# The second attention of a two-block kernel: scores two pairs ahead in an idle accumulator, probabilities normed before their transposes, whole units of projection between pairs

## The chip, the cores and the metric

One core of one Trainium2 chip. The metric is the device time of one execution in microseconds (us), lower is better. Three executions of the kernel before took 921.38, 922.76 and 923.89 us, median 922.76.

## The reference, cut to what matters

Two transformer blocks in float32 run one after the other on 256 tokens of 1024 features. The second one begins with a projection `proj = h @ w_in + b_in` (3584 columns), and has two attentions over it, with 8 query heads and 2 key heads of 64 features each. Both see 256 own tokens and 256 context tokens, so 512 keys.

```python
s = einsum(q, k) * 64 ** -0.5                # 128 queries x 512 keys for each head
# A: windowed, with a sink            B: global
m = max(max(s), sink)                 # p = softmax(s)
e = exp(s - m)
p = e / (sum(e) + exp(sink - m))
o = einsum(p, v)
out = (sigmoid(g_a) * (o_a @ w_branch_a) + sigmoid(g_b) * (o_b @ w_branch_b)) @ w_out
```

The gate logits g_a and g_b are the last 2048 columns of the projection. They are not needed by the attention, so their part of the projection can be computed beside it.

## The kernel before, in words

**Weights and units.** Every weight matrix is walked in panels of 512 columns (`panels`, L84), and a panel in units of 256 rows. For each unit SyncE loads `raw` (a ring of 4), ScalarE rounds it to `whi` (L1411), VectorE subtracts to get `wlo` (L1952), and TensorE multiplies with the two as `unit` (L760) says: 12 matmuls of 128x512 for 256 tokens, high times high, high times low, low times high. ScalarE and VectorE each write their splits into their own instruction order with `ahead(pos)` (L1415, L1957): all splits up to unit pos + 3 that are not yet issued come at this place of the program. Panels alternate between the two accumulators `acc[0]` and `acc[1]` (two PSUM banks each; `Plan.bank`, L119). The first unit of a panel waits until the panel before it in the same accumulator is evacuated (`panel_out`). For the panels IN3 to IN6 (gate logits) VectorE does that in `biased` (L1979), which first calls `ahead` for the panel's last unit.

**The attention stage.** 16 pairs: branch A has pairs 0 to 7, branch B pairs 8 to 15; a pair is two heads times 128 queries. For each pair TensorE makes scores (L1258) into `scores0` and `scores1`, VectorE masks (A alone), takes the maximum and scales it (L2647, L2648, L2651 or L2312), ScalarE takes the exponentials with their sum (L1802 for the sink in A, L1804), TensorE transposes the probabilities (L875), ScalarE copies the transposes out (`t_out`, L1468), and TensorE multiplies them with the values (L1269). Transposes and values use two PSUM banks `turned0` and `turned1` in strict turn: the list `t_names` (L168) gives each use its bank, and a use waits until the one two places before it is copied out (`t_begin`, L805). Before the change the order in that list is, for pair p: PT(2p), PT(2p+1), O(p). Four small matmuls (L1273) broadcast the inverse sums of the pair into the bank of O(p); VectorE copies them out (L2663) and multiplies them into the values (L2664, into `oabT`). After four pairs `oabT` is split into high (ScalarE, L1831) and low (VectorE, L2668) for the panels BA0 to BB1.

**Order of the work.** Each engine's program is written by hand, and each runs in its order. The three functions called `attend_pairs` (L858 TensorE, L1492 ScalarE, L2136 VectorE) hold the loops. Between the pairs TensorE runs one unit per pair of the panels IN3 to IN6, BA0, BA1 (`AB_FILL`), in two halves of 128 tokens (`ab_fill`): one ahead of values(p), one behind. `ab_units(j)` = min(18, j + 2) says how many units are done at pair j; units 18 and 19 come after the loop. `AB_TURNS` names further transposes between pairs: the keys and queries of branch B (kB.0, kB.1, qB.0, qB.1 at pairs 4, 5, 6) and rows of gate1 (pairs 9, 10). GpSimd squares, norms and turns B's queries and keys meanwhile.

Of the kernel before, what the change touches and what calls it, by code (L numbers as in the profile page):

```python
# [100 lines left out]

NARROW = dict(MK0=H_MEM * DQ_MEM, AQ=GATE_RANK + H_MEM * DQ_MEM, CK=KV_RANK + ROPE)


class Plan:


    def __init__(self):
        self.no, self.unit, self.landed, self.cols = {}, {}, [], []
        loads = [0] * RING  # L110
        for i, (name, kts, per_unit) in enumerate(panels()):
            self.no[name], self.unit[name] = i, len(self.landed)
            for u in range(len(self.landed), len(self.landed) + kts // UNIT):
                loads[u % RING] += 16 * per_unit
                self.landed.append(loads[u % RING])
                self.cols.append(NARROW.get(name, COLS))
        self.units = len(self.landed)

    def bank(self, name):  # L119

        return self.no[name] % 2, self.no[name] // 2
# [13 lines left out]
AB_TURNS = {4: ("kB.0",), 5: ("kB.1",), 6: ("qB.0", "qB.1"), 9: ("gate1.0",), 10: ("gate1.1",)}  # L135
MOD_CTX = 4
# [10 lines left out]
AB_LAST = 2  # L147
# [7 lines left out]
def ab_units(j):  # L155

    return min((4 * KT + 2 * KT // 2) // UNIT - AB_LAST, j + 2)

# [9 lines left out]
def t_names():  # L168
# [11 lines left out]
    out += pairs_t("AB", AB_PAIRS, {p: list(v) for p, v in AB_TURNS.items()})  # L180
# [17 lines left out]
def pairs_t(name, n, extra={}, ahead={}):  # L198

    out = []  # L200
    for p in range(n):
        out += [f"{name}.PT{2 * p}", f"{name}.PT{2 * p + 1}"] + ahead.get(p, []) + [f"{name}.O{p}"] + extra.get(p, [])
    return out
# [5 lines left out]
             + [f"MLA.{i}" for i in range(H_MLA)] + [f"AB.{i}" for i in range(2 * HEADS * T)])  # L209
# [30 lines left out]
def hybrid_kernel(nc, a, out):  # L240

    ctx = ExitStack()
    with ctx:
# [15 lines left out]
        sc = [ctx.enter_context(nc.psum_tensor(f"scores{i}", [P, COLS], F32)) for i in range(2)]  # L259

# [120 lines left out]
        oabT = sb("oabT", [P, KT, SEQ], F32, three)  # L381
        inverse_row = sb("inverse_row", [P, P], F32, three)
# [16 lines left out]
        s_full = [sem(f"scores_full{i}") for i in range(2)]  # L399
        s_free = [sem(f"scores_free{i}") for i in range(2)]  # L400
# [56 lines left out]
        def normed(t):  # L457

            room = oabT[:, 4 * t + 2:4 * t + 4, :].rearrange("p a b -> p (a b)")
# [282 lines left out]
        def _(pe):  # L742
# [115 lines left out]
            def attend_pairs(name, n, scores, blocks, values, fill_units, after=None, fill_rest=None):  # L858
# [8 lines left out]
                if fill_rest:  # L867
                    fill_rest(0)
# [9 lines left out]
                for p in range(n):  # L878
                    turned_out(p, 0)
                    if fill_rest:  # L880
                        turned_out(p, 1)
                    if p + 1 < n:
                        score(p + 1)
                    if not fill_rest:
                        turned_out(p, 1)
# [6 lines left out]
                    if fill_rest:  # L892
                        fill_rest(p + 1)
                    if after:
                        after(p)
# [358 lines left out]
            def ab_scores(p, banks):  # L1254
# [3 lines left out]
                return [pe.matmul(banks[e][:, :], qT[br][64 * e:64 * e + 64, hp, P * t:P * t + P],  # L1258
                                  kT[br][64 * e:64 * e + 64, 2 * hp // GROUP, :], start=True, stop=True)
                        for e in range(2)]  # L1260

            def ab_values(p, bank):
                br, hp, t = ab_pair(p)
                group = HD * (2 * hp // GROUP)
                for kt in range(4):
                    v = qkv[:, kt, 768 * br + 640:768 * br + 768] if kt < 2 else \
                        kvx[:, kt - 2, 256 * br + 128:256 * br + 256]
                    for e in range(2):
                        pe.matmul(bank[HD * e:HD * e + HD, 0:P], v[:, group:group + HD],  # L1269
                                  probT[:, e, P * kt:P * kt + P], start=(kt == 0), stop=(kt == 3))  # L1270
                pe.wait_ge(ev("ab_sums"), p + 1)
                for e in range(2):
                    ins = pe.matmul(bank[HD * e:HD * e + HD, P:2 * P],  # L1273
                                       soft[:, (2 * p + e) % 4, 8:9].broadcast_to([P, HD]), ident[:],
                                    start=True, stop=True)
                return ins

            def ab_unit(j, tokens=range(T)):

                if j < 16:  # L1280
                    unit(AB_FILL[j // 4], j % 4, lta, tokens=tokens)
                    return
                if j == 16 and 0 in tokens:
                    lt_wait("oab", 1)
                unit(AB_FILL[4 + (j - 16) // 2], j % 2, ltb, first_kt=2 * (j % 2), tokens=tokens,
                     low=("oab", 1) if j == 16 and 0 in tokens else None)

            def ab_fill(p, tokens):
                for j in range(ab_units(p - 1) if p else 0, ab_units(p)):
                    ab_unit(j, tokens)  # L1290
# [12 lines left out]
            def ab_turn(i, j):  # L1303
                for name in AB_TURNS.get(i, ())[j:j + 1]:
# [8 lines left out]
            def ab_rest(p):  # L1313
                if p > 0:
                    ab_turn(p - 1, 0)
                ab_fill(p, (1,))

            attend_pairs("AB", AB_PAIRS, ab_scores, 4, ab_values, lambda p: ab_fill(p, (0,)), after=lambda p: ab_turn(p, 1),
                         fill_rest=ab_rest)


            ab_unit(18)
# [72 lines left out]
        def _(act):  # L1395
# [96 lines left out]
            def attend_pairs(name, n, exps, first, units, blocks, between=None, after=None):  # L1492
# [11 lines left out]
                for p in range(n):  # L1504
# [6 lines left out]
                    if between:  # L1511
                        between(p)
# [4 lines left out]
                    if after:  # L1517
                        after(p)
# [280 lines left out]
            def ab_exps(i, slot, row, bank):  # L1799
                br, h = i // (HEADS * T), 2 * (i % (HEADS * T) // (2 * T)) + i % 2  # L1800
                if br == 0:
                    act.activation(soft[:, row, 6:7], GAIN["attn_sink_2"][:, h:h + 1], ACT.Exp,  # L1802
                                   bias=soft[:, row, 2:3], scale=-1.0)
                return act.activation(prob[:, slot, :], bank[:], ACT.Exp, bias=soft[:, row, 2:3],  # L1804
                                      scale=HD ** -0.5, accum_out=soft[:, row, 4:5])

            def ab_out(i, j):
                for name in AB_TURNS.get(i, ())[j:j + 1]:
# [8 lines left out]
            def ab_between(i):  # L1817
                if i == 1:
                    sqrt("ab", stat[:, 2:4, :])
                ab_out(i, 0)  # L1820

            def ab_after(i):
                ab_out(i, 1)
                if i % AB_SPAN == 0 and i > 0:
                    oab_hi(i // AB_SPAN - 1)

            def oab_hi(g):

                b, k = T_USE[f"AB.O{AB_SPAN * (g + 1) - 1}"]
                act.wait_ge(t_free[b], k + 2)  # L1830
                act.copy(ltb[0][:, 2 * g:2 * g + 2, :], oabT[:, 2 * g:2 * g + 2, :]).then_inc(lt_hi, 1)  # L1831

            attend_pairs("AB", AB_PAIRS, ab_exps, PLAN.unit["IN3"], ab_units, 4, ab_between, ab_after)
            gate2_sigmoid(0)
            oab_hi(3)
# [94 lines left out]
        def _(dve):  # L1930
# [205 lines left out]
            def attend_pairs(name, n, maxima, sums, weigh, first, units, after=None, early_sums=False,  # L2136
                             before_maxima=None, before_weighing=None):
# [10 lines left out]
                def inverses(p):  # L2148
# [5 lines left out]

                ahead(first)
                softmax(0)
                for p in range(n):
                    if early_sums:
                        inverses(p)
                    ahead(first + units(p))  # L2160
                    if before_maxima:
                        before_maxima(p)
                    if p + 1 < n:
                        softmax(p + 1)
                    if not early_sums:
                        inverses(p)
                    if before_weighing:
                        before_weighing(p)
# [3 lines left out]
                    if after:  # L2172
                        after(p)
# [458 lines left out]
            def norm_sums(t):  # L2632
                for v, s, _, square in normed(t):
# [6 lines left out]
            def ab_step(i):  # L2640
                return i // (HEADS * T), 2 * (i % (HEADS * T) // (2 * T)) + i % 2, i // 2 % T

            def ab_maxima(i, s, bank):
                br, h, t = ab_step(i)
                if br == 0:
                    far = bank[:, P * (1 - t):P * (1 - t) + P]
                    done(dve.tensor_tensor(far, far, (keep_past if t == 0 else keep_next)[:], ALU.add))  # L2647
                done(dve.tensor_reduce(s[:, 0:1], bank[:], AX.X, ALU.max))  # L2648
# [281 lines left out]
```

## Time and profile before

| | |
|---|---|
| median of 3 executions | 922.76 us |
| the profiled execution, its own time | 922.41 us |
| its span in the trace | 920.8 us |
| TensorE (PE) matmul busy | 899.3 us, 98% |
| VectorE (DVE), ScalarE (ACT), GpSimd (POOL) busy | 720.8, 551.3, 162.2 us |
| mean granted TensorE clock | 0.998 |
| attention stage, first scores to the end of unit 19 | 563.80 to 682.95 us |

The span is the time between the first and the last instruction that the profiler recorded; 1.6 us of the execution lie around it. A duration of a matmul contains its way through the array, so matmuls that follow one another overlap in the table: what a group costs is the distance between the start of its first and the start of the next group.

### The profile page before, as it was taken

Reading aid. Unit: us, or ns where it says so; the run is one execution under the profiler, and the core shown is the slowest. Engines: PE = TensorE matmul, PEld = TensorE weight load, DVE = VectorE, ACT = ScalarE, POOL = GpSimd, SP = SyncE. Lnnn points to the kernel's source line nnn. Section 1 sums busy time; section 2 is a strip of 40 time slices with the busy share of each in tenths; the row PEclk is TensorE's granted clock in tenths of the full one; section 3 lists DMA queues with packets and bytes.
Section 4 is the critical chain, followed back from the end, with each engine's and each line's share of the span. In section 5 each row is a group of like instructions: output and inputs, shape, how many; then the busy total and the mean of one; then the engine's idle time right before and its main releaser. Section 6 shows DMA issues by size and latency. Waiting matters only on the chain.

```text
span 920.8 us, 13753 instructions
## 1 busy us (share of the span) xinstructions
PE 899.3 (98%) x4732; PEld 729.8 (79%) x4732; DVE 720.8 (78%) x1046; ACT 551.3 (60%) x863; POOL 162.2 (18%) x247
## 2 busy tenths in 40 slices
PE   8999999999999999999999999999999999999996
PEld 6888888777878778888888887666678688888885
DVE  4779476878878778887779798865668889999976
ACT  6775755476776576777333445755664766666633
POOL 8000000215600000110112001640000023344400
PEclk9999999999999999999999999999999999999999
DMA  9756844876653447887699655322246456555572
GB/s 322 203 151 202 278 138 120 284 275 202 175 177 112 128 143 255 269 287 259 211 330 334 211 177 196 98 80 82 80 148 191 146 179 182 178 171 179 173 245 82
DMA packets 100538, 176.20 MB, mean 191 GB/s; under 512 B 8561, under 2 KB 36593, under 8 KB 100353
## 3 DMA queue, kind: packets, MB, share of 16 engines
q1 hardware_dynamic: 93120, 149.87, 50.7%
q0 software_dynamic: 7184, 25.50, 8.3%
q8 instruction: 34, 0.56, 0.2%
q14 instruction: 24, 0.19, 0.1%
q10 hardware_dynamic: 176, 0.08, 0.0%
HBM read 174.38 MB, written 1.05 MB: 191 GB/s over the span
## 4 chain that ended last, share of the span: by engine, by line
PE 57%; DVE 5%; ACT 2%; issue 1%; DMA 1%; DVEq 0%
PE acc L783 39%; PE acc L1160 3%; PE acc L1165 2%; PE scores L1160 2%; PE turned L1160 2%; PE turned L1269 2%; PE scores L1258 1%; PE turned L875 1%; DVE wlo L1952 1%; PE turned L1371 1%; PE turned L1165 1%; PE scores L1165 1%; PE turned L1185 1%; PE turned L819 1%; DMA raw<-in_w_out 1%
## 5 line engine op out<-in xcount | busy, mean ns | idle before, releaser
L1952 DVE TENSOR_TENSOR wlo<-raw,whi 128x1024 fp32r<-128x1024 f32 (+3 forms) x269 | 346.0, 1306 | 91.0 <-ACT whi L1411 80.7
L1411 ACT CAST whi<-raw 128x1024 fp32r<-128x1024 f32 (+3 forms) x269 | 273.3, 1032 | 150.8 <-PE acc L783 99.6
L783 PE MATMUL acc<-whi,lta 128*128 128x512 f32 (+2 forms) x896 | 227.9, 392 | 0.2 <-DVEq L2529 0.2
L783 PEld LDWEIGHTS acc<-whi,lta 128*128 128x128 f32 x896 | 160.2, 188 | 43.4 <-issue 10.4
L783 PE MATMUL acc<-wlo,lta 128*128 128x512 f32 (+2 forms) x448 | 121.2, 383 | 0.0
L665 POOL DMA_DIRECT2D wm<-in_w_mod x48 | 34.4, 719 | 422.6 <-DVEq L2083 239.7
L783 PEld LDWEIGHTS acc<-wlo,lta 128*128 128x128 f32 x448 | 82.9, 188 | 16.9
L783 PE MATMUL acc<-whi,ltb_hi 128*128 128x512 f32 (+1 forms) x268 | 73.3, 392 | 1.7 <-ACT whi L1411 0.8
L783 PE MATMUL acc<-wlo,ltb_hi 128*128 128x512 f32 (+1 forms) x268 | 71.1, 384 | 1.6 <-DVE wlo L1952 1.6
L783 PE MATMUL acc<-whi,ltb_lo 128*128 128x512 f32 (+1 forms) x268 | 71.5, 385 | 0.1
L783 PEld LDWEIGHTS acc<-wlo,ltb_hi 128*128 128x128 f32 x268 | 49.4, 188 | 12.0 <-DVE wlo L1952 2.0
L783 PEld LDWEIGHTS acc<-whi,ltb_lo 128*128 128x128 f32 x268 | 49.3, 188 | 11.4 <-DVE ltb_lo L2783 1.4
L783 PEld LDWEIGHTS acc<-whi,ltb_hi 128*128 128x128 f32 x268 | 47.8, 188 | 13.2 <-issue 2.7
L724 POOL TENSOR_TENSOR conv<-conv 128x512 f32<-128x512 f32 x6 | 7.8, 1294 | 166.3 <-DVEq L2832 166.3
L1160 PE MATMUL acc<-lta,whi 128*128 128x512 f32 x128 | 35.0, 395 | 0.0
L783 PE MATMUL acc<-whi,ff_hi 128*128 128x512 f32 x128 | 35.0, 395 | 0.0
L783 PE MATMUL acc<-whi,ff_lo 128*128 128x512 f32 x128 | 34.2, 389 | 0.0
L783 PE MATMUL acc<-wlo,ff_hi 128*128 128x512 f32 x128 | 34.2, 389 | 0.0
L1468 ACT ACTIVATE probT<-turned 128x512 f32<-128x512 f32 (+1 forms) x44 | 23.7, 581 | 17.6 <-PE turned L875 11.2
L783 PEld LDWEIGHTS acc<-whi,ff_lo 128*128 128x128 f32 x128 | 24.0, 188 | 5.0
L783 PEld LDWEIGHTS acc<-wlo,ff_hi 128*128 128x128 f32 x128 | 24.0, 188 | 5.0
L2081 DVE SCALAR_TENSOR_TENSOR turn<-wm,sic,turn 128x512 f32<-128x512 f32 x35 | 26.2, 749 | 1.1
(387 smaller groups left out, 1437.0 us busy)
## 6 DMA issues: line engine op xcount, KB each, us to landing
raw<-in_w_in SPq DMA_DIRECT2D x88, 512.0 KB, 4.2
wm<-in_w_mod POOLq DMA_DIRECT2D x48, 512.0 KB, 6.5
raw<-in_w_up SPq DMA_DIRECT2D x88, 256.0 KB, 3.0
raw<-in_w_up SPq DMA_DIRECT2D x32, 512.0 KB, 4.7
raw<-in_w_down SPq DMA_DIRECT2D x32, 512.0 KB, 5.2
raw<-in_w_down SPq DMA_DIRECT2D x44, 256.0 KB, 3.1
raw<-in_w_o SPq DMA_DIRECT2D x8, 512.0 KB, 4.5
raw<-in_w_out SPq DMA_DIRECT2D x8, 512.0 KB, 4.3
```

The lines of the kernel that those rows point to most:

```text
L665: pool.dma_start(wm[:, k], rows(a["w_mod_2"], k)[:, :, bass.ds(COLS * c, COLS)])\
L783: ins = pe.matmul(acc[s][:, t, 0:n], lhs[part][:, kt0 + kk, tok], w[:, u % RING, kk, 0:n], start=(opens and k == 0 and kk == 0 and j == 0) ...
L819: ins = pe.transpose(bank[:, 256 * kk + P * t:256 * kk + P * t + P], src[:, t, c:c + P], ident[:])
L875: ins = pe.transpose(bank[:, P * j:P * j + P], prob[:, e, P * j:P * j + P], ident[:])
L1160: pe.matmul(up_bank(c, f), whi[:, u % RING, kk, P * f:P * f + P], lta_parts[:, :, UNIT * k + kk], start=(k == 0 and kk == 0), stop=False)
L1165: ins = pe.matmul(up_bank(c, f)[:, 0:SEQ], wlo[:, u % RING, kk, P * f:P * f + P], lta_parts[:, 0, UNIT * k + kk], start=False, stop=(k == ...
L1185: ins = pe.matmul(bank[:, 2 * j:2 * j + 1], src[:, P * j:P * j + P], one_col[:], start=True, stop=True)
L1269: pe.matmul(bank[HD * e:HD * e + HD, 0:P], v[:, group:group + HD], probT[:, e, P * kt:P * kt + P], start=(kt == 0), stop=(kt == 3))
L1411: act.copy(whi[:, s, :, 0:n], raw[:, s, :, 0:n]).then_inc(hi_ready, 1)
L1468: act.activation(dst, tb[b][0:(parts or P), 0:n], ACT.Copy, scale=scale).then_inc(t_free[b], 1)
L1952: dve.tensor_tensor(wlo[:, s, :, 0:n], raw[:, s, :, 0:n], whi[:, s, :, 0:n].bitcast(F32), ALU.subtract)\
L2081: done(dve.scalar_tensor_tensor(total, w, factor, total, ALU.mult, ALU.add))
```

## The change

It concerns the attention stage alone.

- Panels IN3 to IN6 and BA0 all go into `acc[0]`. The two banks of `acc[1]` become `scores2` and `scores3`. Scores of pair p use banks 0, 1 or 2, 3 in turn, and are made at pair p - 2; those of pair 1 wait for the evacuation of IN2 from `acc[1]`.
- VectorE multiplies each row of probabilities by its inverse sum in place (`ab_norm`, two `tensor_scalar` of 128x512 for each pair) before TensorE transposes them. The matmuls of L1273, the copy L2663 and the product L2664 go, and so does `oabT`.
- ScalarE rounds O(p) from PSUM to `ltb[0]` (`ab_hi`) and VectorE subtracts to `ltb[1]` (`ab_low`), 128x128 for each pair, in place of four times 128x512.
- values(p-1) comes after the transposes of pair p and the scores of pair p + 2. The order of the `turned` banks becomes PT(2p), PT(2p+1), O(p-1), then extra transposes.
- TensorE runs whole units: `ab_units(j)` = min(19, j + 3).
- `prob` and `probT` get a second copy each.
- The norm sums of B's keys and queries move ahead of the loop, and sqrt("ab") ahead of the copies of pair 0.

```diff
+BESIDE_SCORES = ("IN3", "IN4", "IN5", "IN6", "BA0")
...
+            s = 0 if name in BESIDE_SCORES else i % 2
+            self.banks[name] = s, filled[s]
...
+AB_LATE = 6
-AB_LAST = 2
+AB_LAST = 1
...
-    return min((4 * KT + 2 * KT // 2) // UNIT - AB_LAST, j + 2)
+    return min((4 * KT + 2 * KT // 2) // UNIT - AB_LAST, j + 3)
...
+    for p in range(AB_PAIRS):
+        out += [f"AB.PT{2 * p}", f"AB.PT{2 * p + 1}"] + ([f"AB.O{p - 1}"] if p else []) + list(AB_TURNS.get(p, ()))
...
+        sc += [acc[1][:, t] for t in range(T)]
```

TensorE:

```diff
+            ab_scores(0)
+            s, k = PLAN.bank("IN2")
+            pe.wait_ge(panel_out[s], k + 2)
+            ab_scores(1)
+            ab_fill(0)
+            for p in range(AB_PAIRS):
+                ab_turned(p)
+                if p + 2 < AB_PAIRS and p != AB_LATE:
+                    ab_scores(p + 2)
                 if p > 0:
+                    ab_values(p - 1)
+                ab_turn(p)
+                ab_fill(p + 1)
+                if p == AB_LATE:
+                    ab_scores(p + 2)
+            ab_values(AB_PAIRS - 1)
             ab_unit(19)
```

`ab_turned` waits for `ab_normed` of each head; `ab_values` waits for the copies of its own pair and, in `t_begin`, for its bank.

ScalarE:

```diff
+            ahead(PLAN.unit["IN3"])
+            ab_exp(0)
+            ab_exp(1)
+            sqrt("ab", stat[:, 2:4, :])
+            for p in range(AB_PAIRS):
+                for e in range(2):
+                    t_out(f"AB.PT{2 * p + e}", ab_probT[p % 2][:, e, :])
+                if p > 0:
+                    ab_hi(p - 1)
+                ahead(PLAN.unit["IN3"] + ab_units(p))
+                ab_out(p)
+                if p + 2 < AB_PAIRS:
+                    ab_exp(p + 2)
+            ahead(PLAN.unit["IN3"] + ab_units(AB_PAIRS))
+            ab_hi(AB_PAIRS - 1)
             gate2_sigmoid(0)
```

VectorE (`IN_DONE` is 1, 5, 9, 13 after the change):

```diff
+            def ab_norm(p):
+                for e in range(2):
+                    b, k = S_USE[f"AB.{2 * p + e}"]
+                    dve.wait_ge(s_free[b], k + 2)
+                s = ab_rows(p)
+                if p < AB_PAIRS // 2:
                     done(dve.tensor_tensor(s[:, :, 4:5], s[:, :, 4:5], s[:, :, 6:7], ALU.add))
                 done(dve.reciprocal(s[:, :, 8:9], s[:, :, 4:5]))
+                for e in range(2):
+                    row = ab_prob[p % 2][:, e, :]
+                    dve.tensor_scalar(row, row, s[:, e, 8:9], None, ALU.mult).then_inc(ev("ab_normed"), 1)
...
+            ahead(PLAN.unit["IN3"])
+            ab_maxima(0)
+            norm_sums(0)
+            ab_norm(0)
+            norm_sums(1)
+            var(stat[:, 2:4, :], HD).then_inc(ev("ab_var"), 1)
+            ab_maxima(1)
+            for p in range(AB_PAIRS):
+                if p in IN_DONE:
+                    c = IN_DONE.index(p)
+                    biased(f"IN{3 + c}", gate2[:, :, COLS * c:COLS * c + COLS])
+                if p + 1 < AB_PAIRS:
+                    ab_norm(p + 1)
+                if p == 0:
+                    inverse("ab", stat[:, 2:4, :])
+                    dve.sem_inc(ev("ab_inverse"), 1)
+                ahead(PLAN.unit["IN3"] + ab_units(p))
+                if p == AB_LATE:
+                    ab_low(p - 1)
+                if p + 2 < AB_PAIRS:
+                    ab_maxima(p + 2)
+                if p > 0 and p != AB_LATE:
+                    ab_low(p - 1)
```

## Rows read from the trace of the kernel before

**Rows 1.** The page, parts 1 and 2: busy engines, granted clock in 40 slices.

```profile
PE 899.3 (98%) x4732; PEld 729.8 (79%) x4732; DVE 720.8 (78%) x1046; ACT 551.3 (60%) x863; POOL 162.2 (18%) x247
...
PEclk9999999999999999999999999999999999999999
```

**Rows 2.** The timeline of PE, one pair: start us, us, engine line op, names, shape, count.

```profile
571.42 1.13 PE L1258 MATMUL scores<-kT_a,qT_a 64*128 64x512 f32 x4
572.48 1.20 PE L783 MATMUL acc<-whi,lta 128*128 128x512 f32 x4
...
574.07 0.66 PE L1269 MATMUL turned<-probT,qkv 128*64 128x128 f32 x8
574.56 0.61 PE L1269 MATMUL turned<-probT,kvx 128*64 128x128 f32 x8
574.99 0.39 PE L1273 MATMUL turned<-ident,soft 128*64 128x128 f32 x4
575.31 1.21 PE L783 MATMUL acc<-whi,lta 128*128 128x512 f32 x4
...
576.83 1.03 PE L875 MATMUL turned<-ident,prob 128*128 128x128 f32 x8
577.79 1.13 PE L1258 MATMUL scores<-kT_a,qT_a 64*128 64x512 f32 x4
```

**Rows 3.** The timeline of PE at the stage's two ends (unit 19 begins at 680.23).

```profile
563.80 1.13 PE L1258 MATMUL scores<-kT_a,qT_a 64*128 64x512 f32 x4
...
680.23 1.07 PE L783 MATMUL acc<-whi,ltb_hi 128*128 128x512 f32 x4
...
682.95 1.07 PE L783 MATMUL acc<-whi,ltb_hi 128*128 128x512 f32 x4
```

**Rows 4.** The timeline of DVE, parts of pairs 3 and 9.

```profile
590.39 1.22 DVE L1984 TENSOR_TENSOR gate<-acc,bias 128x1024 f32<-128x1024 f32 x1
591.84 0.25 DVE L2657 TENSOR_TENSOR soft<-soft 128x2 f32<-128x2 f32 x1 [0.22 <-DVE gate L1984]
...
592.44 1.23 DVE L1952 TENSOR_TENSOR wlo<-raw,whi 128x1024 fp32r<-128x1024 f32 x1
593.58 0.29 DVE L2647 TENSOR_TENSOR scores<-scores,keep_past 128x128 f32<-128x128 f32 x1
...
595.95 0.28 DVE L2663 COPY inverse_row<-turned 128x128 f32<-128x128 f32 x1
...
622.29 0.68 DVE L2648 TENSOR_REDUCE soft<-scores 128x1 f32<-128x512 f32 x1
...
623.79 0.15 DVE L2312 TENSOR_SCALAR soft<-soft 128x1 f32<-128x1 f32 x1
```

**Rows 5.** The timeline of ACT.

```profile
578.62 1.28 ACT L1462 ACT_TABLE_LOAD   x1
...
588.96 0.29 ACT L1802 ACTIVATE soft<-gains,soft 128x1 f32<-128x1 f32 x1 [0.22 <-DVE soft L2651]
...
589.73 0.19 ACT L1804 ACTIVATION_READ_ACCUMULATOR prob<-scores,soft 128x1 f32 x1
589.82 1.03 ACT L1411 CAST whi<-raw 128x1024 fp32r<-128x1024 f32 x1
591.11 1.08 ACT L1468 ACTIVATE probT<-turned 128x512 f32<-128x512 f32 x2 [0.26 <-PE turned L875]
```

**Rows 6.** Groups by line and shape: count | busy us, mean ns | idle before.

```profile
L1744 ACT COPY probT<-turned 128x256 f32<-128x256 f32 x8 | 2.7, 398 | 0.0
...
L2079 DVE TENSOR_SCALAR turn<-wm,sic 128x512 f32<-128x512 f32 x5 | 2.4, 481 | 0.0
```

**Rows 7.** The timeline of DVE at the stage's start: first maxima, first norm sum, their variance.

```profile
566.39 0.30 DVE L2647 TENSOR_TENSOR scores<-scores,keep_past 128x128 f32<-128x128 f32 x1
...
575.97 0.67 DVE L2634 TENSOR_REDUCE stat<-oabT 128x8 f32<-128x512 f32 x1
...
578.68 0.18 DVE L2060 TENSOR_SCALAR stat<-stat 128x32 f32<-128x32 f32 x1
```

More of the change, by code:

```diff
@@ L119, in bank @@
     def bank(self, name):
[L121 removed]
+        return self.banks[name]
 PLAN = Plan()
@@ L208 @@
              + [f"gla.{s}.{t}" for s in range(1, 8) for t in range(T)]
-             + [f"MLA.{i}" for i in range(H_MLA)] + [f"AB.{i}" for i in range(2 * HEADS * T)])
+             + [f"MLA.{i}" for i in range(H_MLA)])
+MLA_SCORES = {b: 1 + max(k for c, k in S_USE.values() if c == b) for b in range(2)}
+for i in range(2 * HEADS * T):
+    b = i % 4
+    S_USE[f"AB.{i}"] = b, i // 4 + MLA_SCORES.get(b, 0)
 COLUMNS = (("g_mem", 8), ("g_mix", 8), ("g_ffn", 8), ("g_ckv", 2), ("c_2", 8), ("c_ctx_2", 8),
@@ L1489, in attend, with attend_pairs @@
                         after(i)
-            def attend_pairs(name, n, exps, first, units, blocks, between=None, after=None):
+            def attend_pairs(name, n, exps, first, units, blocks, after):
                 def exp(p):
@@ L1797, in _, with ab_exp, ab_out @@
             keys_out(0)
[L1799 to L1808, printed above, removed]
+            def ab_exp(p):
+                br, hp, _ = p // (HEADS // 2 * T), p % (HEADS // 2 * T) // T, p % T
+                for e in range(2):
+                    g = STEPS["AB"][0] + 2 * p + e
+                    b, _ = S_USE[f"AB.{2 * p + e}"]
+                    row = soft[:, g % 4]
+                    act.wait_ge(soft_ready, g + 1)
+                    if br == 0:
+                        act.activation(row[:, 6:7], GAIN["attn_sink_2"][:, 2 * hp + e:2 * hp + e + 1], ACT.Exp,
+                                       bias=row[:, 2:3], scale=-1.0)
+                    act.activation(ab_prob[p % 2][:, e, :], sc[b][:], ACT.Exp, bias=row[:, 2:3],
+                                   scale=HD ** -0.5, accum_out=row[:, 4:5]).then_inc(s_free[b], 1)
+            def ab_out(p):
+                for name in AB_TURNS.get(p, ()):
                     g = int(name[-1])
@@ L1815, in ab_out, with ab_hi @@
                         queries_out(1, (g,))
[L1817 to L1833, printed above, removed]
+            def ab_hi(p):
+                br, hp, t = p // (HEADS // 2 * T), p % (HEADS // 2 * T) // T, p % T
+                b, k = T_USE[f"AB.O{p}"]
+                act.wait_ge(t_full[b], k + 1)
+                act.copy(ltb[0][:, 4 * br + hp, P * t:P * t + P], tb[b][:, 0:P])\
+                   .then_inc(lt_hi if p % AB_SPAN == AB_SPAN - 1 else ev("oab_hi"), 1)
+            ahead(PLAN.unit["IN3"])
[3 more added lines that the diff above has]
+            for p in range(AB_PAIRS):
+                for e in range(2):
+                    t_out(f"AB.PT{2 * p + e}", ab_probT[p % 2][:, e, :])
[7 more added lines that the diff above has]
+            ab_hi(AB_PAIRS - 1)
             gate2_sigmoid(0)
-            oab_hi(3)
             for n in (1, 2, 3):
@@ L2134, in attend, with attend_pairs @@
                         after(i)
-            def attend_pairs(name, n, maxima, sums, weigh, first, units, after=None, early_sums=False,
-                             before_maxima=None, before_weighing=None):
+            def attend_pairs(name, n, maxima, sums, weigh, first, units, after, before_weighing):
                 def rows_of(p):
@@ L2146, in softmax @@
                         maxima(2 * p + e, rows_of(p)[e], sc[b]).then_inc(soft_ready, 1)
-                def inverses(p):
+                ahead(first)
+                softmax(0)
+                for p in range(n):
+                    ahead(first + units(p))
+                    if p + 1 < n:
+                        softmax(p + 1)
                     for e in range(2):
@@ L2153, in inverses @@
                     sums(p, soft[:, r:r + 2])
[L2155 to L2168, printed above, removed]
+                    before_weighing(p)
                     b, k = T_USE[f"{name}.O{p}"]
@@ L2637, in _ @@
             done(dve.tensor_scalar(GAIN["attn_sink_2"], GAIN["attn_sink_2"], -1.0, None, ALU.mult))
[L2640 to L2648, printed above, removed]
-                if br == 0:
-                    return dve.tensor_scalar(s[:, 2:3], s[:, 0:1], -HD ** -0.5, GAIN["attn_sink_2"][:, h:h + 1],
-                                             ALU.mult, ALU.min)
-                return neg(s, 1, HD ** -0.5)
```

173 lines of the change are left out of this document (83 added, 90 removed).

## The prediction, made before the changed kernel was run

> **What bounds the kernel now.** I read the busy shares first: TensorE's matmuls fill 98% of the span, with the granted clock at its upper level, 2.4 GHz, in all 40 slices [rows 1]. So time is won only where TensorE has less to do or waits less, and each new wait of TensorE goes straight into the time. The timeline of PE then shows what one pair costs: transposes 0.96 us (576.83 to 577.79), scores 1.06, half a unit 1.59, values 0.92, the broadcast of inverse sums 0.32, the other half 1.52; together 6.37 [rows 2]. The groups follow one another without a gap, so the stage, 563.80 to the end of unit 19 at 682.95, is 119.15 us of nearly pure TensorE work [rows 3]. Last I read the timelines of DVE and ACT for the price of their steps [rows 4 to 7]. Neither sets the pace now: VectorE is busy 78% and ScalarE 60% of the span [rows 1].
>
> **What goes.** The broadcast: 16 x 0.32 = 5.1 us of TensorE. Two half units cost 3.11, a whole one 2.72 where units follow one another (680.23 to 682.95) [rows 2, 3]; between other work I give it 2.8, so 16 x 0.3 = 4.8. If TensorE still sets the pace, that is 9.9 us won.
>
> **What comes, and what each step costs.** Scores, maxima, exponentials and transposes keep their counts. New on VectorE for each pair: two scalings of 128x512, 0.48 each in the same form, 0.8 for both as neighbours overlap [rows 6], and the low part of 128x128, priced as the copy of that shape that goes, 0.28 [rows 4]. New on ScalarE: the high part, 128x128 out of PSUM, which no row has. It lies between 0.19, a reading of one column [rows 5], and 0.40, a copy of twice the size [rows 6]; I take 0.27. A handover between engines I take as 0.05, an estimate; the longest in the rows is 0.23 (591.61 to 591.84) [rows 4]. Loads: no DMA is added, moved past another or removed; a load waits for the low split of its slot, four units ahead of its own use, and that stays.
>
> What decides is order. I followed the three programs for one step p, counting what each instruction stands behind:
>
> - ScalarE: copies of PT(2p), PT(2p+1); high(p-1); high split of unit p+5; exponentials p+2.
> - VectorE: norm(p+1); low split of unit p+5; maxima p+2; low(p-1).
> - TensorE: transposes p; scores p+2; values p-1; unit p+3.
>
> Two things follow. High(p-1) waits for values(p-1), and the split queued behind it on ScalarE needs nothing of it but comes later by it; VectorE's low split waits for that one, and the maxima are queued behind the low split. And the bank of O(p-1), freed by low(p-1) behind the maxima, is the one that the second transposes of pair p+1 write. That closes a ring with one turn for each pair: second transposes 0.48, scores 1.06, values 1.10 until their last result (574.07 to 575.17) [rows 2], handover 0.05, high part 0.27, high split 1.03 [rows 5], handover 0.05, low split 1.14, maxima of branch A 2.37 (593.58 to 595.95), low part 0.28 and 0.1 to free the bank [rows 4]: **7.9 us for each pair, where it takes 6.37 now**. In branch B the maxima need no mask and no sink: 1.6 (622.29 to the end of the second scaling) [rows 4], so 7.2. Making scores two pairs ahead doesn't open the ring, since the transposes two places further need a bank of this one.
>
> **The evacuations.** With all gate panels in one accumulator, units 4, 8, 12 and 16 wait for the evacuation of the panel that ended just before. `biased` stands in steps 1, 5, 9, 13, and its own `ahead` puts the low split of unit p+5 ahead of it. So from the start of values: 1.10, high part, high split, low split, 1.22 of evacuation [rows 2, 4, 5] are 4.9, against 0.92 of values that TensorE has to do: a wait of 4.0 at each. Then norm(p+1), which else hides in the wait for ScalarE, comes behind it: 1.45 to the next instruction [rows 4] and 1.2 (B: 1.0) for the norm make these steps 10.6 and 9.6.
>
> **The start.** VectorE: first maxima from 566.39 [rows 7] to 568.8; three norm sums, half of 575.97 to 578.68 [rows 7], 570.1; norm of pair 0, 571.3; the other sums, 572.8; maxima of pair 1, 575.2. ScalarE: the exponentials, 0.95 for the second head (588.96 to 589.92), 576.2; table load 1.28 and root 0.2, 577.7; two copies 1.1, 578.8; high split of unit 3, 579.8 [rows 5]. Low split, 581.0. TensorE has done two scores, three units, the transposes of pair 0 and scores 2 by 576.7 and waits 4.3 for unit 3. Splits 3 to 5, maxima, exponentials and the copy that frees the bank of values(0) end at 587.4, and there values(0) begin.
>
> **The sum.** Values to values: step 1 10.6; 7.9; 7.9; 8.4 with a key copy of 0.5 on ScalarE; step 5 10.6; then the late scores, where queries turned wait for low(5) (4.1 behind values), a unit, scores 8, their maxima, exponentials and a copy follow one another, 11.8: 57.2. Branch B: 7.2, 7.2, 10.1 (step 9, with a gate copy), 7.7, 7.2, 7.2, 9.6, and two steps without maxima, 5.3 and 3.9: 65.4. So values(15) begin at 587.4 + 57.2 + 65.4 = 710.0, and unit 19 ends 3.6 later, 713.6 in place of 682.95: +30.7. Behind it, the merge of BA0 now frees the accumulator of BB0 and waits for the first gate sigmoid, queued behind high(15): from 711.4, table load 1.28, sigmoid 1.06 (as a 128x1024 split), merge 1.22, 715.0: +1.3. Sum: **+32 us**. The profiled execution took 922.4, its span 920.8 and 1.6 around it, and stands 0.3 below the median: 922.4 + 32 = 954.
>
> GpSimd's squares and norms start no later than now, since the root comes earlier, and end before the keys are wanted; if they were late, pair 4 would wait instead of running in the ring.
>
> **Rivals.** *The ring doesn't bind and TensorE sets the pace: faster.* It decides if splits run ahead of the values they are queued behind, for example if the cursor of `ahead` stands one unit further than I count. For it: TensorE's own work falls to about 5.8 for a pair, under all that VectorE has (maxima 2.37, split 1.14, norm 1.2, low 0.3: 5.0). Against it: the order is in the program. 922.4 - 9.9 + 0.5 (scores 1 wait for IN2) = 913.
>
> *Only the start, the four evacuations and the late scores wait, ordinary steps don't:* 4.3 + 4 x 4.0 + 4 - 9.9 = +14, so 937. The same cursor, wrong in one place only.
>
> *The ring, and the clock on top.* Here TensorE would stand still about 4 us five times. The page's clock line shows no slice below the upper level, and no row has a standstill of that length, so no row prices it. If it fell to 1.2 GHz at all five and each took one unit of 2.72 [rows 3] at half speed, that adds 13.6: 968. The Trainium skill (TensorE: Matmul & The Clock Gate, "HAM oscillation — how this bites in real kernels") warns that gaps in which TensorE idles bring its clock down. By that rule the time would be 968; no run shown here can bear it out.
>
> *No change within 0.3%* (about what a measurement of this kernel can tell): the gain of 9.9 would have to meet losses of the same size; no mechanism of mine gives that.
>
> **How the numbers follow.** Ring with evacuations, 0.73, 954, own range 948 to 961: the high part between its bounds moves 14 steps by -1.1 to +1.8, handovers of 0.1 add 4, overlaps I missed take 5. Clock on top 0.10; only the single waits 0.06; faster 0.09; same 0.02. The range 944 to 968 takes in the first two, with some room below for waits that are partly hidden, and leaves out the other three, 0.17. Faster 0.09, same 0.02, slower 0.89.
>
> **What would show it.** In the trace of the changed kernel: scores of neighbouring pairs 7.9 apart in A and 7.2 in B; PE idle before the second transposes (2.0 in A, 1.3 in B, ended by VectorE's low part); before unit 3 (by a split) and before units 4, 8, 12, 16 (by the evacuation), about 4 each; in all some 40 us of PE idle in the stage, and VectorE waiting for `whi`, ScalarE for O(p-1). Pairs 5.8 apart without idle time would prove the ring wrong; long matmuls behind the 4 us waits would be the clock.

## The result, and the profile after

The changed kernel takes 965.14 us (median of 4 executions, 962.28 to 967.48), the kernel before on the same chip 922.75 (4 executions, 921.38 to 923.89): **slower by 4.6%**, ratio 1.0456, 95% interval 1.0439 to 1.0473. The forecast was 954, its range 944 to 968. So the sign and the range held, and the size is nearer to the rival with the clock on top (968) than to the likeliest case. That case, the ring without the clock, had a range of its own, 948 to 961, and the run lies outside it; the wider range held because it took in the rival.

The page of the changed kernel, its span and its parts 1 and 2, against [rows 1]:

```profile
span 964.5 us, 13613 instructions
...
PE 910.3 (94%) x4668; PEld 740.3 (77%) x4668; DVE 729.1 (76%) x1058; ACT 553.5 (57%) x875; POOL 162.6 (17%) x247
...
PE   8999999999999999999999997777889999999996
...
PEclk9999999999999999999999997888989999999998
```

TensorE has 64 matmuls fewer and yet 11 us more busy time, and its share falls from 98% to 94%. Of the six slices in a row in which it is busy 7 or 8 tenths, five show the granted clock below the upper level; before, no slice did [rows 1]. Two losses lie in the same stretch: TensorE waits, and it is slow behind the waits.

The waits of PE in the stage (what waited, for whom: us in total, times, longest):

```profile
PE turned L1273 <- DVE ltb_lo L2701: 10.4, 8, 1.9
PE acc L796 <- DVE gate L2010: 9.9, 3, 3.7
PE acc L796 <- issue: 3.8, 1, 3.8
PE turned L1287 <- ACT probT_odd L1486: 3.7, 3, 2.3
PE acc L796 <- ACT whi L1429: 3.0, 1, 3.0
PE turned L1238 <- DVE ltb_lo L2701: 2.3, 1, 2.3
```

The first row is the ring of the prediction: second transposes behind the low part. The next two are the four evacuations (the fourth, before unit 16, has no releaser in the records, but VectorE's evacuation of IN6 ended just before it, at 704.4), the fourth row is values behind their copies (2.26 of it before values(0)), the fifth the start, the last the late scores. They sum to 33 us, where the prediction had 40.

The timeline of PE of one turn of the ring in branch B, against [rows 2]:

```profile
656.48 0.63 PE L1273 MATMUL turned<-ident,prob 128*128 128x128 f32 x4 [1.03 <-DVE ltb_lo L2701]
657.04 1.13 PE L1264 MATMUL scores<-kT_b,qT_b 64*128 64x512 f32 x4
658.10 0.66 PE L1287 MATMUL turned<-probT_odd,qkv 128*64 128x128 f32 x8
...
663.63 0.63 PE L1273 MATMUL turned<-ident,prob_odd 128*128 128x128 f32 x4 [1.01 <-DVE ltb_lo L2701]
664.19 1.13 PE L1264 MATMUL acc<-kT_b,qT_b 64*128 64x512 f32 x4
```

Scores follow scores after 7.15 us (657.04 to 664.19), where the prediction had 7.2 and the kernel before 6.37. In branch A the turn from 599.30 to 607.24 took 7.94 with the clock up (7.9 said); the two after it took 9.11 and 8.38, with slow matmuls in them. The other engines in the same turn, ACT and then DVE, against [rows 5] and [rows 4]:

```profile
659.24 0.27 ACT L1843 CAST ltb_hi<-turned 128x128 fp32r<-128x128 f32 x1 [1.32 <-PE turned L1287]
659.40 1.05 ACT L1429 CAST whi<-raw 128x1024 fp32r<-128x1024 f32 x1
```

```profile
660.48 1.23 DVE L1978 TENSOR_TENSOR wlo<-raw,whi 128x1024 fp32r<-128x1024 f32 x1 [2.32 <-ACT whi L1429]
661.62 0.68 DVE L2670 TENSOR_REDUCE soft<-scores 128x1 f32<-128x512 f32 x1
...
663.13 0.15 DVE L2327 TENSOR_SCALAR soft<-soft 128x1 f32<-128x1 f32 x1
663.20 0.28 DVE L2701 TENSOR_TENSOR ltb_lo<-turned,ltb_hi 128x128 fp32r<-128x128 f32 x1
```

Read in order of time the ring closes: values from 658.10, high part at 659.24, high split, low split at 660.48, maxima, low part at 663.20, transposes at 663.63. ScalarE stood idle 1.32 us and VectorE 2.32 in it: no engine is full, all three take turns.

Then two of the four evacuations, the timeline of PE before units 8 and 12, and unit 16 behind the fourth:

```profile
632.17 3.52 PE L796 MATMUL acc<-whi,lta 128*128 128x512 f32 x8 [3.12 <-DVE gate L2010]
...
636.46 1.03 PE L1273 MATMUL turned<-ident,prob 128*128 128x128 f32 x8
...
670.04 3.78 PE L796 MATMUL acc<-whi,lta 128*128 128x512 f32 x8 [3.12 <-DVE gate L2010]
...
675.33 1.47 PE L1273 MATMUL turned<-ident,prob 128*128 128x128 f32 x8
...
704.52 2.04 PE L796 MATMUL acc<-whi,ltb_hi 128*128 128x512 f32 x4 [3.75 <-issue]
...
709.78 1.32 PE L1273 MATMUL turned<-ident,prob 128*128 128x128 f32 x8
```

A unit took 4.3 us (632.17 to 636.46) and twice 5.3, where one at full speed takes 2.72 [rows 3]. The same in stretches (us; busy time of each engine with its instructions; then the granted clock):

```profile
577.00:584.00 7.00, 4.03 (x11) 3.17 (x12) 5.26 (x6) 6.08 (x8) 5.15 (x5) 0.76 0.11 18
...
650.00:660.00 10.00, 8.01 (x60) 5.86 (x61) 5.04 (x12) 5.80 (x14) 0.00 (x0) 1.00 0.16 53
670.00:680.00 10.00, 9.96 (x47) 7.47 (x48) 3.81 (x11) 3.71 (x8) 0.00 (x0) 0.69 0.15 51
680.00:700.00 20.00, 16.81 (x108) 11.47 (x108) 10.89 (x24) 10.78 (x24) 0.00 (x0) 1.00 0.23 79
```

In 670 to 680 TensorE is busy all the time and gets 47 matmuls done at 0.69; in 650 to 660 it is busy 8 of 10 us and does 60 at 1.00.

The stage's end, the timeline of PE, against [rows 3]:

```profile
721.72 1.20 PE L796 MATMUL acc<-whi,ltb_hi 128*128 128x512 f32 x4
...
725.90 1.16 PE L796 MATMUL acc<-whi,ltb_hi 128*128 128x512 f32 x4 [1.17 <-issue]
```

Unit 19 begins at 721.72, and with its 2.72 ends at 724.4, 41.5 us later than the 682.95 of before; the wait for the accumulator of BB0 behind it is 1.17 (1.3 said). Together 42.7, which is the whole difference of the medians, 42.4.

### The profile page after: what moved, and what is told of

It reads as the page before. It is cut to its first block, busy times and chain, and to the rows that moved or that the text cites. A ratio compares the mean times of both kernels' runs of the same rounds, so it can differ in the third digit from the quotient of the medians.

```text
span 964.5 us, 13613 instructions
## 1 busy us (share of the span) xinstructions
PE 910.3 (94%) x4668; PEld 740.3 (77%) x4668; DVE 729.1 (76%) x1058; ACT 553.5 (57%) x875; POOL 162.6 (17%) x247
## 4 chain that ended last, share of the span: by engine, by line
PE 53%; DVE 8%; ACT 4%; issue 2%; DMA 1%; DVEq 0%; ACTq 0%
PE acc L796 37%; PE acc L1164 3%; DVE wlo L1978 3%; PE turned L1287 2%; ACT whi L1429 2%; DVE soft L2670 2%; PE acc L1169 2%; PE scores L1164 2%; PE turned L1164 2%; PE turned L1273 1%; PE turned L1389 1%; PE turned L1169 1%; PE scores L1169 1%; PE scores L1264 1%; PE acc L1264 1%
## 5 line engine op out<-in xcount | busy, mean ns | idle before, releaser
L796 PE MATMUL acc<-whi,lta 128*128 128x512 f32 (+2 forms) x896 | 231.3, 400 | 13.2 <-DVE gate L2010 9.9
L796 PEld LDWEIGHTS acc<-whi,lta 128*128 128x128 f32 x896 | 166.6, 194 | 49.7 <-DVE gate L2010 10.7
L796 PEld LDWEIGHTS acc<-whi,ff_hi 128*128 128x128 f32 x128 | 23.4, 188 | 4.4
```

What stands on the lines that cost most here:

```text
L796: ins = pe.matmul(acc[s][:, t, 0:n], lhs[part][:, kt0 + kk, tok], w[:, u % RING, kk, 0:n], start=(opens and k == 0 and kk == 0 and j == 0) ...
```

## The experiments

All are edits of the changed kernel. The first four ran beside 7 executions of the kernel before (median 922.87), the other four beside 9 (923.58).

**The high split ahead of the high part.** The ring says that the split on ScalarE comes late only because it stands behind a wait for values(p-1). Here it is moved ahead of that wait, still behind the copies.

```diff
                     t_out(f"AB.PT{2 * p + e}", ab_probT[p % 2][:, e, :])
+                ahead(PLAN.unit["IN3"] + ab_units(p))
                 if p > 0:
                     ab_hi(p - 1)
-                ahead(PLAN.unit["IN3"] + ab_units(p))
```

> Edit: ScalarE's high split of the next unit stands ahead of high(p-1) in each step; nothing else. Ring theory: the high split no longer waits for values(p-1), so about 1.3 us drop out of the ring (values to the high part, 1.10 + 0.05 + 0.27, are then beside the split). Ordinary pairs 6.7 apart in branch A and 5.9 in B (7.9 and 7.2 in the changed kernel), waits before units 4, 8, 12, 16 of 2 to 3 us in place of 3.1 to 3.7. The stage ends 17.5 us earlier, and with shorter waits some of the clock's share of about 10 us comes back: 939 to 948 in all. Rival (the added work on VectorE, the two scalings of each pair, sets the pace): VectorE's program is untouched, so no change, 965. Rival (only the five single waits cost): ordinary pairs keep their distance, at most 4 us come back.

Measured: 940.84 (940.11 to 941.30), 1.0196 of before, interval 1.0179 to 1.0213. One line moved takes back 24 us. Waits of PE in the stage:

```profile
PE turned L1287 <- ACT probT_odd L1486: 4.9, 3, 3.5
PE acc L796 <- DVE gate L2010: 4.5, 3, 1.7
PE turned L1273 <- DVE ltb_lo L2701: 3.4, 4, 1.4
```

The low part's 10.4 fell to 3.4 and the evacuations' 9.9 to 4.5. One place in a queue fed both. The 24 us are the ring and the clock together: the same 4668 matmuls kept TensorE busy for 897.5 us here and for 910.3 in the changed kernel.

**The high split first in the step**, ahead of the copies too.

```diff
             for p in range(AB_PAIRS):
+                ahead(PLAN.unit["IN3"] + ab_units(p))
                 for e in range(2):
                     t_out(f"AB.PT{2 * p + e}", ab_probT[p % 2][:, e, :])
                 if p > 0:
                     ab_hi(p - 1)
-                ahead(PLAN.unit["IN3"] + ab_units(p))
```

> Edit: ScalarE's high split of the next unit stands first in each step, ahead of the copies of the transposes, as in the kernel before. Ring theory: the split waits for nothing of this step. Pairs 5.9 apart in both branches (TensorE's own work), waits before units 4, 8, 12, 16 under 1 us, what is left are the start (3 to 5 us) and the late scores (10.6 for that pair). The stage ends 26 us earlier, the clock stays up nearly everywhere: 926 to 934. Rival (VectorE's added work sets the pace): no change, 965. Rival (one accumulator for all gate panels is what costs): the waits before units 4, 8, 12, 16 stay over 3 us and the gain stays under 15.

Measured: 933.98 (933.37 to 934.48), 1.0121, interval 1.0104 to 1.0138. The timeline of PE, scores of three neighbouring pairs:

```profile
661.20 1.13 PE L1264 MATMUL acc<-kT_b,qT_b 64*128 64x512 f32 x4
...
667.13 1.13 PE L1264 MATMUL scores<-kT_b,qT_b 64*128 64x512 f32 x4
...
673.06 1.13 PE L1264 MATMUL acc<-kT_b,qT_b 64*128 64x512 f32 x4
```

These pairs of branch B are 5.93 apart, with no idle time: less than the 6.37 of before. This is the gain that the prediction gave the change if TensorE set the pace (5.8). In B it exists; the order of ScalarE's program hid it. In A the ordinary pairs are 6.5 to 7.3 apart, where 5.9 was expected in both branches.

**The evacuation first.** `biased` of IN3 to IN6 without the split of its own `ahead`; ScalarE as in the changed kernel.

```diff
 # in biased(): the wait for the panel's last unit, without ahead()
+                if name in BESIDE_SCORES:
+                    dve.wait_ge(unit_used, RING + last_unit(name) + 1)
+                    p, n = acc[PLAN.bank(name)[0]], n_gate[name]
+                else:
+                    p, n = panel_wait(name), n_gate[name]
-                p, n = panel_wait(name), n_gate[name]
```

> Edit: the evacuation of IN3 to IN6 no longer puts VectorE's low split of the next unit ahead of itself. Ring theory: the evacuations run in the time in which VectorE waits for ScalarE's split, the waits before units 4, 8, 12, 16 go, and the ordinary pairs stay 7.9 and 7.2 apart. Stage 10 us shorter by the waits; the clock, which fell after these waits, stays up, another 5 to 9: 945 to 951. Rival (one accumulator is the cost whatever the order, since the evacuation takes 1.2 us between two units): waits over 1 us stay, gain under 5.

Measured: 950.93 (949.53 to 951.82), 1.0303, interval 1.0283 to 1.0322. Waits of PE in the stage:

```profile
PE turned L1273 <- DVE ltb_lo L2705: 17.1, 12, 2.2
```

No unit waits for `gate` any more, but 12 transposes now wait for the low part where 8 did, 6.7 us more in all. The steps with an evacuation have become ordinary turns of the ring. 14 us come back.

**TensorE kept busy in the long waits.** The scores of pair p + 2 are made four times in steps 0, 1, 5, 9 and 13, the same numbers written each time, so 60 more matmuls stand where TensorE would idle. (`ab_scores` gets two switches for it, `first` and `last`: whether it waits for its banks and whether it announces the scores.) If time is lost to the wait alone, this costs or changes nothing; if the clock behind it costs, it comes back.

```diff
+                again = p in (0, 1, 5, 9, 13)
                 if p + 2 < AB_PAIRS and p != AB_LATE:
-                    ab_scores(p + 2)
+                    ab_scores(p + 2, last=not again)
                 if p > 0:
                     ab_values(p - 1)
                 ab_turn(p)
+                for n in range(3 if again else 0):
+                    ab_scores(p + 2, first=False, last=n == 2)
```

> Edit: in steps 0, 1, 5, 9, 13 the scores of pair p + 2 are made four times over, three of them in the wait of about 4 us that follows, and announced after the last; results the same. TensorE has 15 more pairs of score matmuls, 16 us of work, all inside the five long waits. Clock theory: the clock stays at the upper level, units behind the waits take 2.8 us and not 4 to 5, and the time falls to about 955 (the 954 of the sum without the clock). Rival (the long matmuls behind the waits are no clock but late operands or an artefact): no gain, 965 or more. If announcing the scores later is on the path, up to 2 us of the gain are lost.

Measured: 958.82 (956.52 to 962.03), 1.0383, interval 1.0359 to 1.0407: 6.3 us less than the changed kernel, by doing more. The timeline of PE at the first two long waits, and at the one before unit 12:

```profile
580.06 2.11 PE L796 MATMUL acc<-whi,lta 128*128 128x512 f32 x8 [0.47 <-ACT whi L1436]
...
588.85 0.66 PE L1291 MATMUL turned<-probT,qkv 128*64 128x128 f32 x8 [3.54 <-ACT probT_odd L1493]
...
590.15 4.22 PE L1266 MATMUL acc<-kT_a,qT_a 64*128 64x512 f32 x12
594.29 2.11 PE L796 MATMUL acc<-whi,lta 128*128 128x512 f32 x8
...
671.91 2.11 PE L796 MATMUL acc<-whi,lta 128*128 128x512 f32 x8 [0.35 <-DVE gate L2017]
```

The first two units are at full speed, the eight high matmuls in 2.11 where the changed kernel needed 3.23 and 3.78. Where TensorE still stood, 3.54 before values(0), it was slow behind it: twelve scores took 4.22, against 1.06 for four at full speed [rows 2]. In branch B, where the repeated scores filled the two long waits, values 8 to 9 took 10.0 us and values 12 to 13 took 9.1; the changed kernel took 12.5 and 11.8, and the sum of the prediction, which has no clock in it, says 10.1 and 9.6. That 6.3 us came back and not the 10 that were expected has its place in branch A: there the clock fell in three ordinary turns, behind waits of 2.37, 1.83 and 1.90, and values 1 to 4 took 28.6 us where the changed kernel took 26.1.

**Both orders**, the second and the third edit together.

> Edit: the two orders of before together: ScalarE's high split first in each step, and the evacuation without the low split ahead of it. Ring theory: stage 3 us shorter than with the first alone (933.98), since the waits of 1 us before units 4 and 16 and their followers go; 928 to 932, and still above the kernel before, because the start (about 5 us) and the late scores (about 4) are paid whatever the order, which eats the 10 us that TensorE's lighter pairs give. Rival (the lighter pairs win once nothing waits): under 920.

Measured: 931.55 (930.77 to 933.48), 1.0084, interval 1.0071 to 1.0098. Of the third edit's 14 us only 2.4 are left once the split is early (3.4 by the ratios, since the two runs stood beside other executions of the kernel before): the two edits take away the same lateness.

**Both orders, and the start mended.** What is left stands at the start and at the late scores: values(0) waited 5.2 us in the run above. Here the exponentials of pairs 2 and 8 go behind the copies of the next step, the root to step 1 with its inverse, and the gate sigmoid of BA0 one step earlier.

```diff
-            sqrt("ab", stat[:, 2:4, :])
+            late = (0, AB_LATE)
...
                     t_out(f"AB.PT{2 * p + e}", ab_probT[p % 2][:, e, :])
+                if p - 1 in late:
+                    ab_exp(p + 1)
...
+                if p == 1:
+                    sqrt("ab", stat[:, 2:4, :])
-                if p + 2 < AB_PAIRS:
+                if p + 2 < AB_PAIRS and p not in late:
                     ab_exp(p + 2)
+                if p == AB_PAIRS - 2:
+                    gate2_sigmoid(0)
...
-            gate2_sigmoid(0)
```

> Edit: as both orders together, and besides: in steps 0 and 6 ScalarE's exponentials of pair p + 2 move behind the copies of step p + 1; the root for B's norms moves to step 1; the first gate sigmoid moves ahead of the last pair's copies. Ring theory: the first values begin 5 us earlier, values 6 some 2 us, and the wait of 1.2 us before BB0 goes. By the same adding of steps the stage ends within 1 us of the kernel before: 921 to 926, verdict same. Rival (something of the change costs that is no order, e.g. contention on PSUM or SBUF): 928 or more, with matmuls or copies longer than in the kernel before.

Measured: 928.36 (927.65 to 929.98), 1.0055, interval 1.0042 to 1.0069. Better by 3.2, and 2 above what was expected. The timeline of PE shows where, and the stretches beside it how the clock went:

```profile
592.19 1.09 PE L1273 MATMUL turned<-ident,prob 128*128 128x128 f32 x4 [3.39 <-DVE ltb_lo L2710]
593.21 2.08 PE L1264 MATMUL scores<-kT_a,qT_a 64*128 64x512 f32 x4
```

```profile
589.00:592.00 3.00, 0.00 (x0) 0.00 (x0) 2.86 (x8) 1.08 (x4) 2.77 (x4) 1.00 0.39 106
592.00:596.00 4.00, 3.81 (x20) 2.00 (x22) 3.03 (x6) 2.76 (x6) 3.61 (x6) 0.57 0.30 117
```

The wait has moved from values(0) to the second transposes of pair 2, behind the low part of pair 0: VectorE is busy 2.86 of the 3.00 us, so here it does set the pace. The kernel is still slower than before by 0.55%.

The rival of this run, a cost that is no order, had 928 or more, and its time came. Its sign, longer matmuls or copies, came in part. The copies of the transposes last 0.60 us as in the kernel before, but VectorE's instructions are longer where GpSimd works beside them, on the norms of B's keys and queries. The timeline of DVE in this run:

```profile
578.29 3.49 DVE L1983 TENSOR_TENSOR wlo<-raw,whi 128x1024 fp32r<-128x1024 f32 x3
...
587.37 2.12 DVE L1983 TENSOR_TENSOR wlo<-raw,whi 128x1024 fp32r<-128x1024 f32 x1
```

The three low splits took 3.49 us with GpSimd idle from 577 to 584; the single one took 2.12, where 1.22 is usual, with GpSimd busy 2.06 of the 2.50 us from 587 to 589.5. This split stands in front of the low part that the transposes wait for. It is a reading of the trace: no run moved GpSimd's work and nothing else.

**No scalings.** The 32 products of probabilities by inverse sums are left out, so the output lacks the division by the sums; the waits and signals stay. A rival says that VectorE's added work (0.88 for each pair, 14 us) is what costs.

```diff
-                    dve.tensor_scalar(row, row, s[:, e, 8:9], None, ALU.mult).then_inc(ev("ab_normed"), 1)
+                    dve.sem_inc(ev("ab_normed"), 1)
```

> Edit to the changed kernel: the 32 scalings of probabilities on VectorE are left out (the probabilities are used without the division by their sum). Ring theory: they lie in the time in which VectorE waits for ScalarE's split; they count only at the start and in the steps with an evacuation, about 2.5 us together: 960 to 964. Rival (VectorE's added work sets the pace): 16 x 0.8 to 0.9 = 13 to 14 us less, about 951.

Measured: 965.28 (961.38 to 966.89), 1.0456, interval 1.0440 to 1.0472, the ratio of the changed kernel. VectorE is busy 715.0 us in place of 729.1, and the time is the same within the spread of the executions, which is 5.5 us; the 1 to 5 us that were expected for the start and the evacuations can't be told from it. The rival's 14 us are not there: the scalings lie beside the ring, as costed.

**The low part ahead of the maxima.** If the bank of O(p-1) alone were the ring, freeing it earlier would open it. The ring theory has a second arm: maxima p+2 still wait for the low split, and values p+1 need what comes of them.

```diff
-                if p == AB_LATE:
+                if p > 0:
                     ab_low(p - 1)
                 if p + 2 < AB_PAIRS:
                     ab_maxima(p + 2)
-                if p > 0 and p != AB_LATE:
-                    ab_low(p - 1)
```

> Edit to the changed kernel: VectorE's low(p-1) stands ahead of the maxima of pair p + 2 in every step, so the bank that the second transposes need is free 2.4 us earlier; nothing else. Ring theory: no real gain, since the ring has a second arm that is almost as long: maxima, exponentials, first copy of the transposes (on ScalarE behind them), values. Pairs stay 7.5 to 7.9 apart in A, 7.1 in B; TensorE's wait moves from the second transposes to the values; 963 to 966. Rival (only the freed bank binds): ordinary pairs 2 us shorter, 10 waits of 1 to 2 us gone, 945 to 950.

Measured: 960.88 (957.68 to 963.86), 1.0391, interval 1.0369 to 1.0414. 4.3 us won (6.0 by the ratios), more than the 2 at most that were expected, and not the fifteen and more of the single bank. Waits of PE in the stage:

```profile
PE turned L1287 <- ACT probT_odd L1486: 11.3, 8, 3.5
...
PE turned L1287 <- ACT probT L1486: 5.0, 5, 1.7
```

The waits for the low part are gone, and the values wait in their place, 16.3 us for copies of transposed probabilities. Ordinary values in B are 6.8 to 7.1 us apart (7.15 in the changed kernel).

## Why the prediction was right, and where its size was off

**The ring: right, in place and in size.** Scores 7.15 apart in B (7.2 said), twice in a row, and 7.94 in A where the clock stayed up (7.9 said); the waits before the second transposes 1.0 in B (1.3 said) and 1.4 to 1.9 in A (2.0 said); the high part 0.27, the value taken; both scalings 0.88 (0.8 taken, beside other work); the low part 0.28. Moving one split ahead of one wait took back 24 us with VectorE's program untouched, and removing 14 us of VectorE's work took back nothing that can be measured. So the cause is the order of the queues, and the rival in which TensorE sets the pace fails here by 52 us (913 against 965), though its pace of 5.8 for a pair is real in B once the order is changed (5.93 measured).

**The single waits: right in place, a little long.** Before unit 3: 3.05 (4.3 said). Before units 4, 8, 12, 16: 3.70, 3.12, 3.12 and 3.75 (4.0 said of each). Values(0) began at 588.77 (587.4 said). That only these waits count (937) was wrong: with the evacuations taken out of TensorE's way the kernel still took 951.

**The term that was mis-sized is the clock.** The main sum gave it nothing, since "no row has a standstill of that length, so no row prices it". Step by step, from values to values, the sum against the trace:

| step | said | measured | granted clock there |
|---|---|---|---|
| values 6 to 8, two turns in B | 14.4 | 14.3 | full |
| values 9 to 12, three turns | 22.1 | 21.9 | full |
| values 13 to 15, no maxima | 9.2 | 9.3 | full |
| values 0 to 1, evacuation | 10.6 | 11.6 | falls |
| values 1 to 4, three turns in A | 24.2 | 26.1 | falls twice |
| values 4 to 5, evacuation | 10.6 | 11.4 | falls |
| values 5 to 6, late scores | 11.8 | 13.1 | falls |
| values 8 to 9, evacuation | 10.1 | 12.5 | falls |
| values 12 to 13, evacuation | 9.6 | 11.8 | falls |

Where the clock stays up, seven steps, 45.7 us were said and 45.4 measured. All of the excess of the steps, 9.6 us, lies in the others; with 1.4 at the start it makes the 11 by which the run exceeds the forecast of 954.

The 1.4 at the start are a second term, and not the clock: TensorE had finished scores 3 and stood 2.26 us before values(0). The sum took the three low splits there at 1.14 each, 3.4 in all. The timeline of DVE:

```profile
579.95 4.82 DVE L1978 TENSOR_TENSOR wlo<-raw,whi 128x1024 fp32r<-128x1024 f32 x3 [1.55 <-ACT whi L1429]
```

They took 4.82, and GpSimd was busy 5.15 of the 7 us from 577 to 584; with the root moved to step 1 it was idle there and the same three took 3.49. The prediction asked only whether GpSimd would be late, not what its earlier work would lie beside.

Back to the clock. The rival took each unit behind a long wait at half speed, +2.72, five times, 13.6. Measured, to the start of what follows: units 3, 4, 8, 12 and 16 took 4.4, 4.8, 4.3, 5.3 and 5.3, so 10.5 more than five at 2.72, and some of that lies beside other work or is made up by waits that came out shorter than 4.0. Another check needs no path: the changed kernel and the one with the start mended run the same 4668 matmuls, with PE busy 910.3 and 894.3 us. So 16 us of TensorE's busy time are slower work and no more of it. The four executions agree: mean granted clocks of 0.978, 0.978, 0.983 and 0.986 go with 967.48, 966.12, 964.17 and 962.28 us. That the time on the path follows the clock is shown by the scores made four times, which gave back 6.3 us and brought the two steps of branch B down to what the sum had said; that all 9.6 are its doing is read from the table, not tried by itself.

The chance of 0.10 for this rival was too low. That a row is missing for a standstill of 4 us was taken as a reason to count it as nothing, where it only left the price open between 0 and 13.6. The Trainium skill (TensorE: Matmul & The Clock Gate, "HAM oscillation — how this bites in real kernels") says that a kernel whose TensorE idles in gaps loses its clock; this case's trace agrees, with 0.76 granted in 577 to 584 and 0.69 in 670 to 680.

**The stage's end.** BB0 waited 1.17 (1.3 said), and with the sigmoid one step earlier not at all.

**What stays open.** In which order the changed kernel would beat the one before was not found. The best run stands 5 us above it: its steady pairs in B gain 0.44 each (6.37 to 5.93), and the start and the late scores, where scores two pairs ahead have yet to fill the pipeline, lose more than that. An order that also removes the 3.39 before the transposes of pair 2 was not tried, and neither was one that keeps GpSimd's norms away from VectorE's splits.

## What to carry to other kernels

When work is reordered, write out what each engine's program stands behind, and follow one buffer round until it comes back: the ring's length is the time of a turn, whatever the busy shares say. Put what feeds a later step (a split of weights four units ahead) in front of an instruction that waits for the present one, not behind it. And a new standstill of TensorE can cost twice, the wait and the slow work behind it, as most of those of 1.8 us and more did here; if no row prices the second, let the forecast reach to half speed for what follows each of them.

## What the runs showed of the hardware

That short waits suffice was not expected. In the changed kernel scores behind a wait of 1.87 took 1.84, and their values 1.12 where 0.66 is full speed (timeline of PE; this wait and that of 2.27 before turned queries):

```profile
623.73 1.07 PE L1273 MATMUL turned<-ident,prob_odd 128*128 128x128 f32 x8 [1.87 <-DVE ltb_lo L2701]
624.73 1.84 PE L1264 MATMUL acc<-kT_a,qT_a 64*128 64x512 f32 x4
626.49 1.12 PE L1287 MATMUL turned<-probT,qkv 128*64 128x128 f32 x8
...
641.78 0.83 PE L1238 MATMUL turned<-ident,work 128*128 128x128 f32 x4 [2.27 <-DVE ltb_lo L2701]
642.26 3.58 PE L796 MATMUL acc<-whi,lta 128*128 128x512 f32 x8
```

In branch B the waits of 1.0, one in each turn, left the clock at 1.00 (650 to 660 and 680 to 700). Where the fall comes differs too. In the run with the start mended the granted clock was 1.00 while TensorE stood from 589 to 592 with no matmul, and 0.57 in the 4 us of work after it. In the changed kernel it fell inside the wait of 3.70 before unit 4, with no matmul running (the same columns as for the stretches above):

```profile
591.00:592.00 1.00, 0.00 (x0) 0.00 (x0) 0.86 (x1) 0.11 (x1) 0.92 (x2) 0.50 0.00 0
```

It fell inside the waits before units 12 and 16 as well, and only behind the one of 3.05 before unit 3. So a stretch at 1.00 in a wait does not say that the work behind it will be fast.
